# A transformer of two blocks on one core: squares summed on TensorE, one split moved ahead of the root, a map's mixing in two steps, and a later gated branch

## What is computed

```python
for l in range(2):                          # stages 0 and 2, 1 and 3
    u = rms_norm(h, norm_mix_pre[l])
    a, b, c, d, gates = split(u @ w_in[l])
    # a: differential attention, p0 - lam * p1 of two softmax maps
    # b: gated linear attention, both directions
    # c: latent attention with rotary keys; d: windowed attention
    merged = sum(branch_n @ w_branch[l, n] * sigmoid(gate_n))
    h = h + rms_norm(merged @ w_out[l], norm_mix_post[l])
    f = conv_ffn(rms_norm(h, norm_ffn_pre[l]), ...)
    h = h + rms_norm(f, norm_ffn_post[l])
for l in range(2):                          # stages 4 to 9
    h = h + 0.5 * swiglu(h); h = h + mixer_l(h); h = h + 0.5 * swiglu(h)
return rms_norm(h, final_norm)              # stage 10
```

## Time and profile before

| | us |
|---|---|
| median of 3 runs | 2217.5 (2216.9 to 2217.7) |
| the profiled execution, its own time | 2219.3 |
| its span | 2217.5 |
| PE busy | 2170.4 (98%) |
| DVE busy | 1518.6 (68%) |
| ACT busy | 1195.0 (54%) |
| POOL busy | 306.2 (14%) |

### The profile page before, as it was taken

One profiled execution on the slowest core, in us unless ns is written; L12 is line 12 of the kernel. 1 busy time (PEld: TensorE's weight loads), 2 busy tenths in 40 slices (PEclk: granted clock), 3 DMA queues, 4 the chain that ended last, 5 costly groups with the idle time before them and its releaser, 6 DMA issues.

```text
span 2217.5 us, 43378 instructions
## 1 busy us (share of the span) xinstructions
PE 2170.4 (98%) x17567; PEld 2086.2 (94%) x17567; DVE 1518.6 (68%) x2614; ACT 1195.0 (54%) x2053; POOL 306.2 (14%) x285
## 2 busy tenths in 40 slices
PE   7999999999999999999999999999999999999998
PEld 6889989899998999899999999989999999989998
DVE  5776686887477576778856656776665665886654
ACT  4555456665455554566655444455454444665443
POOL 1000112100111001130002210001220220222211
PEclk9999999999999999999999999999999999999999
DMA  7334335355643354454554655435555555435553
GB/s 239 112 126 145 128 115 180 118 176 178 212 130 108 112 150 133 126 184 144 185 187 166 230 183 184 139 115 172 189 182 184 188 186 186 151 126 165 187 185 130
DMA packets 97815, 356.61 MB, mean 161 GB/s; under 512 B 10848, under 2 KB 12000, under 8 KB 97488
## 3 DMA queue, kind: packets, MB, share of 16 engines
q1 hardware_dynamic: 95328, 342.47, 47.8%
q0 software_dynamic: 2000, 10.38, 1.7%
q10 hardware_dynamic: 288, 0.99, 0.1%
HBM read 352.68 MB, written 1.12 MB: 160 GB/s over the span
## 4 chain that ended last, share of the span: by engine, by line
PE 87%; DVE 8%; ACT 2%; issue 1%; DMA 1%; POOL 0%; SPq 0%; DVEq 0%; ACTq 0%; POOLq 0%
PE pd L1318 26%; PE pd L1329 25%; PE pd L1326 25%; DVE wlo L2186 2%; PE pt L1454 1%; PE pd L1470 1%; ACT whi L1761 1%; DMA raw<-in_w 1%; DVE xl L2196 1%; PE ps L1429 1%; PE ps L1663 1%; PE ps L1318 1%; PE pd L1576 1%; PE pd L1484 1%; PE ps L1442 0%
## 5 line engine op out<-in xcount | busy, mean ns | idle before, releaser
L1318 PE MATMUL pd<-xh,whi 128*128 128x256 f32 (+2 forms) x3368 | 986.8, 293 | 2.7 <-DVE tb L2679 1.1
L1761 ACT ACTIVATE whi<-raw 128x1024 fp32r<-128x1024 f32 x618 | 651.1, 1055 | 598.9 <-PE pd L1329 572.7
L1329 PE MATMUL pd<-xh,wlo 128*128 128x256 f32 (+2 forms) x3353 | 953.0, 284 | 7.8 <-DVE wlo L2186 7.8
L1326 PE MATMUL pd<-xl,whi 128*128 128x256 f32 (+2 forms) x3353 | 952.1, 284 | 2.4 <-DVE xl L2196 2.4
L2186 DVE TENSOR_TENSOR wlo<-raw,whi 128x1024 fp32r<-128x1024 f32 x618 | 768.4, 1245 | 262.6 <-ACT whi L1761 260.5
L1318 PEld LDWEIGHTS pd<-xh,whi 128*128 128x128 f32 x3368 | 636.5, 189 | 28.6 <-issue 20.3
L1329 PEld LDWEIGHTS pd<-xh,wlo 128*128 128x128 f32 x3353 | 633.7, 189 | 9.3 <-DVE wlo L2186 9.3
L1326 PEld LDWEIGHTS pd<-xl,whi 128*128 128x128 f32 x3353 | 632.3, 189 | 5.8 <-DVE xl L2196 3.2
L1329 PE MATMUL pd<-ah,wlo 128*128 128x256 f32 (+1 forms) x992 | 280.6, 283 | 0.0
L1326 PE MATMUL pd<-al,whi 128*128 128x256 f32 (+1 forms) x992 | 279.6, 282 | 0.0
L1318 PE MATMUL pd<-ah,whi 128*128 128x256 f32 (+1 forms) x992 | 279.3, 282 | 0.0
(11 more groups left out here) (366 smaller groups left out, 3025.4 us busy)
## 6 DMA issues: line engine op xcount, KB each, us to landing
raw<-in_w SPq DMA_DIRECT2D x648, 512.0 KB, 3.6
TA<-scr POOLq DMA_DIRECT2D x2, 1392.0 KB, 10.8
C<-in_c POOLq DMA_DIRECT2D x1, 2432.0 KB, 11.7
TD<-scr POOLq DMA_DIRECT2D x2, 1056.0 KB, 7.7
TD<-scr POOLq DMA_DIRECT2D x2, 768.0 KB, 12.5
h<-in_h SPq DMA_DIRECT2D x4, 272.0 KB, 7.4
out<-u SPq DMA_DIRECT2D x8, 128.0 KB, 1.8
C<-in_c POOLq DMA_DIRECT2D x1, 800.0 KB, 6.0
```

The costliest lines, as they stand in the source:

```text
L1318: e.matmul(out, hi, xh, start=begin, stop=False)
L1326: e.matmul(out, hi, xl, start=False, stop=False)
L1329: last = e.matmul(out, lo, xh, start=False, stop=end)
L1761: e.activation(m.whi[i][:, 0:n], m.raw[c % NRAW][:, 0:n], ACT.Copy).then_inc(*self.up("ac_hi", ("hi", c)))
```

## The change

`summed_at_once` is true for the squares of h at the entry of the two convolution stages. There all eight squares go to the ring `sq`, POOL's six additions fall away, and PE sums each square on its own (`sum_part`), one within the blocks of each k. At the same entries chunk c0+6 is split at c0+1. `a_mix` becomes `a_scale` and `a_mix`, 0.35 chunks apart. Branch b begins at `gk[0].end + 2.4`.

```diff
+def summed_at_once(name, stage):
+    return name == "h" and (STAGES[stage + 1][0] == "conv_ffn")
...
@@ split_ahead
                 more[c] = c0, room
+            if self.chunks[c0][0][0].x == "x" and STAGES[self.chunks[c0][0][0].key[0]][0] == "conv_ffn":
+                self.split_at[c0 + LEAD + NMORE] = c0 + 1
...
@@ norm_root
-        self.hold("pt", t - 0.01, t + 0.5, ("sum", stage))
-        self.step("pe", t, "sum_acc", stage)
-        self.step("pe", t + 0.01, "sum_last", stage)
+        if summed_at_once("h", stage - 1):
+            self.hold("pt", t - 2.5, t + 0.5, ("sum", stage))
+            for k in range(8):
+                self.step("pe", t - 0.375 * (6 - k) - 0.24 if k < 7 else t, "sum_part", stage, k)
+        else:
+            self.hold("pt", t - 0.01, t + 0.5, ("sum", stage))
+            self.step("pe", t, "sum_acc", stage)
+            self.step("pe", t + 0.01, "sum_last", stage)
...
@@ squares (Plan)
+        if summed_at_once(name, stage):
+            self.hold("sq", t, t + 0.6, (name, stage, k))
+            self.step("ac", t, name + "_sq", stage, k)
+            return
...
@@ mixer
-            self.step("dv", t + 2.7, "a_mix", l, h)
+            self.step("dv", t + 2.7, "a_scale", l, h)
+            self.step("dv", t + 3.05, "a_mix", l, h)
...
-        t = gk[0].end + 1.6
+        t = gk[0].end + 2.4
...
+    def sum_part(self, stage, k):
+        e, m, (_, at), key = self.e, self.m, entering(stage), ("h", stage - 1, k)
+        for s in self.ahead(("h_sq", stage - 1, k), self.free("pt", ("sum", stage)) if k == 0 else None):
+            e.wait_ge(*s)
+        e.matmul(self.buf("pt", ("sum", stage))[:, at], m.c0("ones"), self.buf("sq", key)[:, at],
+                 start=k == 0, stop=k == 7).then_inc(
+            *self.up("pe_norm", ("free", "sq", key), *([("sum", stage)] if k == 7 else [])))
...
@@ squares (Scalar)
-        ring, key = ("sq", (name, stage, k)) if k else ("acc", (name, stage))
+        ring, key = ("sq", (name, stage, k)) if k or summed_at_once(name, stage) else ("acc", (name, stage))
```

More of the change, by code:

```diff
@@ L1271, in run @@
         steps = {
-            "block": self.block, "fill": self.fill, "block_low": self.block_low, "sum_acc": self.sum_acc, "sum_last": self.sum_last,
+            "block": self.block, "fill": self.fill, "block_low": self.block_low, "sum_acc": self.sum_acc, "sum_last": self.sum_last, "sum_part": self.sum_part,
             "post_acc": self.post_acc, "post_last": self.post_last, "v_turn": self.v_turn, "bias": self.bias,
@@ L2159, in run @@
             "c_pad": self.c_pad, "zero_queries": self.zero_queries, "d_pad": self.d_pad, "lam_dots": self.lam_dots, "lam_sum": self.lam_sum,
-            "two_max": self.two_max, "c_max": self.c_max, "c_zero": self.c_zero, "a_mix": self.a_mix,
+            "two_max": self.two_max, "c_max": self.c_max, "c_zero": self.c_zero, "a_scale": self.a_scale, "a_mix": self.a_mix,
             "weights": self.weights, "turned": self.turned, "weighed": self.weighed, "head_mul": self.head_mul,
@@ L2397, in c_max, with a_scale @@
             *self.up("dv_max", ("max", key)))
-    def a_mix(self, l, h):
+    def a_scale(self, l, h):
         e, m = self.e, self.m
         one, two = ("a", l, h, 0), ("a", l, h, 1)
-        P0, P1, s0, s1 = self.buf("P", one), self.buf("P", two), self.buf("st", one), self.buf("st", two)
+        P0, s0, s1 = self.buf("P", one), self.buf("st", one), self.buf("st", two)
         for s in self.ahead(("exp", two), ("lam", l)):
@@ L2413, in a_mix @@
         i.then_inc(*self.up("dv_small", ("a_first", l, h)))
+    def a_mix(self, l, h):
+        e, one, two = self.e, ("a", l, h, 0), ("a", l, h, 1)
+        P0, P1, s1 = self.buf("P", one), self.buf("P", two), self.buf("st", two)
         for s in self.ahead(("a_first", l, h)):
```

## The result

The changed kernel takes 2213.08 us in the median of 17 runs (2209.64 to 2215.64), the kernel before, beside it on the same chip, 2218.55 (2215.75 to 2222.31). The ratio is 0.9976, with a 95% interval of 0.9969 to 0.9982: faster by 0.24%. The forecast was 2210.7, with a range of 2207.0 to 2215.3.

What follows compares the result with a forecast made beforehand. PE, busy 98% of the span, bounds the kernel: only its waits, added instructions or clock count. Gains of 1.7 + 1.7 + 1.1 + 1.2 = 5.7 us, plus 1.1 for the clock, took 2217.5 to 2210.7 us; range 2207.0 to 2215.3.

Steps and rivals of the forecast that it cites:

- Sums: Entries of stages 1 and 3: without GpSimd's additions xl comes sooner, so the last sum starts 1.7 us earlier in each.
- The price (0.455): Convolution entries: one added sum costs PE 0.455 us at stage 1's width; twelve added sums are 5.5 us.
- the pace (1.58 per k: Stage 1's entry: nine matmuls and a sum take PE 1.58 us per k, against DVE's 1.24.
- If DVE did not get faster at all: Stage 1's entry, DVE not faster: the last square would end at 409.10 and the gain still be about 1.5 us.
- Split: Low half moved into DVE's idle time ahead of the root: 1.13 us of PE's waits gone in stage 3, 0 in stage 1.
- Mixing: Stage 2: the low half PE awaits for 3.08 us goes ahead of three additions, so PE goes on 1.24 us earlier.
- they find it done: Stage 2: turns needing the mixed map come some 22 matmuls later and find it done at about 713.4.
- Branch: Later gated branch: four small matmuls come a block later, nothing else on PE; 0, between -0.3 and +0.4 us.
- Clock: Shorter waits in stages 1 and 2 leave fewer low-clock stretches: +1.1 us, between -3.4 and +3.6.
- The base: Starting time of the kernel before, from which the forecast gain was subtracted: the median of its runs, 2217.5 us.

Runs made afterwards that it cites:

- the kernel with early z: The kernel with early sums, plus the first two chunks of z made ahead of the first product's scaling; 2211.80 us against 2217.57 before, ratio 0.9970.
- the two with idle additions: The changed kernel plus six unread GpSimd additions in each convolution entry, with one operand or two different ones; one execution each, 2215.59 and 2216.45 us.
- the kernel with early sums: The changed kernel with the sums of k=6 and 7 right behind that of k=5 on TensorE; 2210.67 us against 2217.32 before, ratio 0.9972.

## Why the prediction was right

- **Sums, 1.7 us an entry.** Measured 1.53 and 1.51. The price (0.455) and the pace (1.58 per k, seen 1.59) held. The 0.2 us that are missing are PE's: from the xl of k=1 to the last sum it took 9.52 us (400.72 to 410.24), busy all the time, where the sum had 9.36; of that, 0.1 is the step behind the first matmul (400.72 to 400.95, 0.23 and not 0.125). One sentence of this step was wrong: "If DVE did not get faster at all ... the gain would still be about 1.5". With DVE slowed as before, 0.39 us remains. I had set the last sum by the last square; PE's blocks ahead of it need xl, which is late by then.
- **Split, 1.13 us in stage 3 and 0 in stage 1.** In stage 3 exactly 1.13 (14.00 to 12.87), and the move into DVE's idle time cost nothing. In stage 1 the 0 holds only with a low stretch of the clock; at full clock it is 1.13 too.
- **Mixing, 1.24 us.** The stall fell by 1.26. But "they find it done" and the silence on the next low half hold only while PE runs at 1.2 GHz behind the stall. At full clock 1.6 us of waits follow, and the part alone gives 0.8 (0.3 to 1.3). The sum took what one wait gave and left out what DVE's full queue takes of it.
- **Branch, 0 within -0.3 and +0.4.** The medians agree, the fit says 0.9 us faster; open.
- **Clock, +1.1 us.** This term is not borne out. The 17 runs after had a mean granted clock of 0.9965, the 73 runs of before beside the experiments 0.9973; at 1.12 us per 0.001 that is 0.9 us lost and not 1.1 won. Against the 17 runs of before beside the change it is open, since their clocks are not on record: they are slower than the 73 (mean 2218.97 against 2217.82), so there the clock may have cost nothing. I read one execution's low stretches as before's own. Behind the roots shorter waits were indeed followed by fewer of them (last section), but there are others elsewhere. The trace after has three as well, at 21.2, 168.0 and 710.7 us; that of before has them at 415.7, 712.7 (the longest) and 760.5.
- **The sum.** At equal clock the change is 5.9 us faster (5.5 to 6.3); the forecast without its clock term was 5.7. The parts alone add up to 1.7 + 2.1 + 0.8 + 0.9 = 5.5. So the forecast is right, and in part by luck, since errors of both signs met: the second split (+1.1) was missing, and so was what the sums and the mixing lose elsewhere (the sums alone give 1.7 of the 3.0 us of their entries, the mixing 0.8 of 1.24). The 2.4 us between 2210.7 and 2213.1 are mostly the clock term: with 5.9 us gained and 0.9 lost, 2217.5 becomes 2212.5. The base was sound: the 2217.5 of three runs agrees with the median of the 73 (2217.57), and the 17 runs beside the change, 2218.55, are the high ones (five over 2220, against four of the 73).
- **What can be told apart.** The prediction held that under 0.2% a measurement of this kernel shows nothing. With 17 runs on each side the interval was 0.9969 to 0.9982, so a difference of 0.1% could be told.

## What to carry to other kernels

Where two engines slow each other, moving the work of one to an engine that has waits can pay even at a bottleneck at 98%: the time comes from the third engine's speed, and idle copies of the removed work show how much. Measure a local edit from a fixed instruction to a fixed instruction, at full clock, and price the total only over many runs; here the stretches repeat to 0.04 us, and the 17 totals after lie 6 us apart. A wait taken out of a full queue is worth what the next ones in line leave of it.

## What the runs showed of the hardware

The clock falls without a wait. In the kernel with early z, PE is busy for all of 743 to 753 us, at full clock, and then at half:

```profile
743.00:753.00 10.00, 10.00 (x115) 9.33 (x115) 6.13 (x19) 2.83 (x5) 0.00 (x0) 1.00 0.30 91
753.00:757.00 4.00, 4.00 (x47) 3.88 (x45) 1.15 (x2) 1.49 (x3) 0.00 (x0) 0.57 0.19 69
```

Of the 115 matmuls there 70 are small (64 or 16 rows, 16 to 128 columns). Nine of the fourteen traces have a low stretch at this place of the program, in stage 2 (before, at 760 us) or in stage 0 (after, at 168 us); the others do the same work at full clock. So what makes it fall is not shown. Behind the root it fell less often where the wait ahead of the first z matmul was shorter: after waits of 1.70 to 1.75 us in five of eight stretches, after 1.35 to 1.38 in four of fourteen, after 0.70 or none in none of six. These are few cases, and elsewhere in the program it fell all the same.

A low stretch costs little where PE is about to wait: behind stage 1's root 13.93 us becomes 14.16, but 12.80 becomes 14.15; behind stage 3's 14.00 becomes 14.01, but 12.87 becomes 13.55. So a kernel with fewer waits pays more for it.

In these entries VectorE is slowed by an addition on GpSimd only where its instruction starts second. From the entry of stage 1 before:

```profile
399.94 0.43 DVE L2225 TENSOR_TENSOR u<-u,rs 128x272 f32<-128x272 f32 x1
400.05 0.95 POOL L2930 TENSOR_TENSOR acc<-acc,sq 128x272 f32<-128x272 f32 x1 [0.34 <-ACT sq L1802]
400.40 0.90 DVE L2232 TENSOR_TENSOR h<-h,u 128x272 f32<-128x272 f32 x1
```

The first instruction was already running when the addition began and keeps its 0.43 us; the third starts within the addition and takes 0.90 in place of 0.44. In six traces with such additions (before, three of the single parts, the two with idle additions), at both entries, each of u, h and xl that starts while one runs takes 0.72 to 1.02 us, and each of the others 0.41 to 0.50. So the order of the starts decides which of them is slow.

Three sums in a row cost what three single ones do. Taken as the prediction took one, from the first sum to the block matmul after next (406.98 to 408.48) less one step of 0.125, they are 1.375 us in the kernel with early sums, 0.46 each.
